# Differential attention of a two-model kernel: the next pair's row maxima directly behind a pair's normalisations on VectorE

## The reference

```python
def diff_attend(q, k, v, lam):
    s = jnp.einsum("bhmqd,bhmkd->bhmqk", q, k).astype(jnp.float32) * (DIFF_QK_DIM ** -0.5)
    p = jax.nn.softmax(s, axis=-1)
    w = (p[:, :, 0] - lam * p[:, :, 1]).astype(v.dtype)
    return jnp.einsum("bhqk,bhkd->bhqd", w, v)
```

## Time and profile before

| | us |
|---|---|
| median of 3 runs | 2204.16 |
| lowest, highest run | 2200.81, 2211.51 |
| the profiled execution's own time | 2201.68 |
| its span in the trace | 2199.8 |
| TensorE busy, share of the span | 2100.1, 95% |
| VectorE busy | 1562.9, 71% |
| ScalarE busy | 1031.1, 47% |
| GpSimd busy | 312.9, 14% |
| mean granted TensorE clock | 0.991 |

### The profile page before, as it was taken

The page is one execution under the profiler, slowest core; times in us unless marked ns, Lnnn a source line. Parts: engine busy times, 40 slices in busy tenths (PEclk is TensorE's granted clock), DMA queues, the critical chain, the costliest instruction groups (busy, mean ns, idle before and its releaser), DMA issues.

```text
span 2199.8 us, 41515 instructions
## 1 busy us (share of the span) xinstructions
PE 2100.1 (95%) x17009; PEld 1973.0 (90%) x17009; DVE 1562.9 (71%) x2072; ACT 1031.1 (47%) x1238; POOL 312.9 (14%) x292
## 2 busy tenths in 40 slices
PE   7899999899899999999999889999999988999998
PEld 6676898799899999999999878999999987899998
DVE  8988657688787655655579988675556998875554
ACT  4112636554664543534545556563355446544332
POOL 3762003200210100100201220110010122000000
PEclk9999999999999999999999999999999999999999
DMA  8688766665445565555666433555555642345552
GB/s 258 226 296 302 256 243 218 219 186 186 122 133 173 188 194 189 176 191 191 200 184 194 129 97 107 176 174 191 188 176 179 186 142 85 108 154 172 181 182 77
DMA packets 292260, 397.42 MB, mean 181 GB/s; under 512 B 9270, under 2 KB 257292, under 8 KB 285452
## 3 DMA queue, kind: packets, MB, share of 16 engines
q1 hardware_dynamic: 285620, 383.53, 53.4%
q0 software_dynamic: 3008, 5.56, 1.1%
q10 hardware_dynamic: 3480, 6.18, 0.8%
HBM read 387.53 MB, written 3.15 MB: 178 GB/s over the span
## 4 chain that ended last, share of the span: by engine, by line
PE 77%; DVE 13%; issue 3%; ACT 3%; DMA 2%; POOL 1%; DVEq 0%; SPq 0%; ACTq 0%; POOLq 0%
PE L L941 63%; PE M L941 4%; DVE w_rest L454 3%; PE L L1222 2%; PE L L1208 2%; PE M L1476 1%; PE L L1235 1%; DVE work L2783 1%; PE L L1291 1%; DMA raw<-in_w_in 1%; POOL m L862 1%; DMA gate<-in_mem 1%; ACT w_high L448 1%; DVE n_rest L2204 1%; PE M L1075 1%
## 5 line engine op out<-in xcount | busy, mean ns | idle before, releaser
L941 PE MATMUL L<-n_high,w_high 128*128 128x256 f32 x3104 | 875.7, 282 | 15.7 <-DVE w_rest L454 10.0
L941 PE MATMUL L<-n_rest,w_high 128*128 128x256 f32 x3104 | 865.9, 279 | 0.0
L941 PE MATMUL L<-n_high,w_rest 128*128 128x256 f32 x3104 | 865.9, 279 | 0.0
L454 DVE TENSOR_TENSOR w_rest<-raw,w_high 128x2048 fp32r<-128x2048 f32 x293 | 673.7, 2301 | 215.6 <-PE L L941 200.6
L448 ACT ACTIVATE w_high<-raw 128x2048 fp32r<-128x2048 f32 x293 | 561.1, 1916 | 342.6 <-PE L L941 316.1
L941 PEld LDWEIGHTS L<-n_high,w_high 128*128 128x128 f32 x3104 | 587.1, 189 | 33.3 <-issue 17.7
L941 PEld LDWEIGHTS L<-n_high,w_rest 128*128 128x128 f32 x3104 | 586.3, 189 | 0.0
L941 PEld LDWEIGHTS L<-n_rest,w_high 128*128 128x128 f32 x3104 | 584.8, 188 | 0.0
L941 PE MATMUL L<-hid_high,w_high 128*128 128x256 f32 x768 | 214.4, 279 | 4.2 <-DVEq L2689 4.2
L941 PE MATMUL L<-hid_high,w_rest 128*128 128x256 f32 x768 | 213.7, 278 | 0.0
L941 PE MATMUL L<-hid_rest,w_high 128*128 128x256 f32 x704 | 195.8, 278 | 0.0
(11 more groups left out here) (426 smaller groups left out, 2962.0 us busy)
## 6 DMA issues: line engine op xcount, KB each, us to landing
raw<-in_w_in SPq DMA_DIRECT2D x116, 1024.0 KB, 5.5
raw<-in_w_ffn SPq DMA_DIRECT2D x99, 1024.0 KB, 5.3
raw<-in_w_ada SPq DMA_DIRECT2D x32, 1024.0 KB, 6.6
raw<-in_w_out SPq DMA_DIRECT2D x16, 1024.0 KB, 4.9
raw<-in_w_gate SPq DMA_DIRECT2D x11, 1024.0 KB, 5.4
raw<-in_w_up SPq DMA_DIRECT2D x11, 1024.0 KB, 5.4
raw<-in_w_down SPq DMA_DIRECT2D x11, 1024.0 KB, 4.9
work<-in_w_ada SPq DMA_DIRECT2D x8, 1024.0 KB, 7.3
```

The lines of the kernel that those rows point to most:

```text
L454: nc.vector.tensor_tensor(w_rest[:, u.first % 2, :], raw[:, u.first % 4, :], w_high[:, u.first % 4, :].bitcast(F32), ALU.subtract).then_in ...
L941: ins = mm(dst, a, b, start=first and i == 0, stop=last and i == 2, skip_group_check=skip)
```

## The change

```diff
                     if kind_of(key) == "diff":
                         if x["whole"]:
-                            for y in tasks[i + 1:i + 3]:
+                            turned_rest(x)
+                        else:
+                            for y in tasks[i + 2:i + 4]:
                                 negative_max(key, y)
-                            turned_rest(x)
```

## The result

The changed kernel takes **2226.56 us** (median of 4 runs, 2225.57 to 2230.45), the kernel before 2206.05 beside it (4 runs): ratio 1.0096, 95% interval 1.0072 to 1.0121, some 20.5 us slower. The profiled execution took 2227.25, its span is 2225.5. Forecast were 2218, in a range from 2208 to 2227, so the time lies at its upper end: 20.5 us more than before, where the sum had 14.2. The sign and the places were right, the size was not.

What follows compares the result with a forecast made beforehand. VectorE's order was taken to set the pace inside differential attention stages. Terms of 8.6 + 3.6 + 2.0 = 14.2 us on the profiled 2201.7 gave 2215.9, and 2.5 us more for the median gave 2218, range 2208 to 2227.

Steps and rivals of the forecast that it cites:

- What bounds, and where it goes: Differential attention stages: VectorE's order can set the pace; maxima moved ahead of their scores make VectorE and what follows wait.
- Pair 1, 2.0 + 2.9 + 3.7 = 8.6: `conv_centre` behind pair 1's maxima starts late by 2.0 us in c0diff, 2.9 in x0diff, 3.7 in x1diff.
- Pair 2, 1.15 + 1.2 + 1.2 = 3.6: `w_rest`, head copy and `conv_scale` behind the maxima delay head 1's values: 1.15 us in c0diff, 1.2 per 512-key stage.
- The term on the overlap with GpSimd: Pair 2: later `conv_scale` leaves part of its overlap with GpSimd's subtractions, giving back 0.5 us per 512-key stage.
- Pairs 4 and 5, 0.65 in each: `w_rest` behind the maxima makes head 2's values 0.65 us later in each stage, 2.0 us in all.
- Pair 0, nothing: `w_rest` behind two maxima costs nothing; pair 1's exponentials start 2.2 us sooner but gain nothing.
- The clock, "I count 0 net": Slow clock behind new waits before the second sums, set against head 2's shorter wait: 0 net, 5 us as the end.
- Rival (a): The clock also falls behind the new waits: +5 us, 2223; chance 0.20.
- The reason given for a return: Head 2's wait gets shorter, since 2.3 us of waiting moved ahead of it, and such a wait can cost clock.
- Rival (b): Only `conv_centre`'s delay arrives, partly absorbed; pairs 2 to 5 cost nothing: +7 us, 2211; chance 0.18.
- Rival (c): Exponentials are the pace, and `w_rest` leaves their chain at pairs 0, 4, 5: 8 us faster, 2196; chance 0.06.

Runs made afterwards that it cites:

- f2: Kernel before with only pair 1's maxima directly behind its normalisations, so that only `conv_centre` goes behind them: ratio 1.0058, three stages +14.0 us.
- g1: Changed kernel with extra matmuls that fit inside TensorE's waits behind the turnings of pairs 1 and 4: ratio 1.0070 to the kernel before, three stages +15.0 us.
- g2: Kernel before with early maxima in pair 2 alone: ratio 1.0032, three stages +8.4 us.
- h1: Kernel before with early maxima in pairs 4 and 5 alone: ratio 1.0025, three stages +11.3 us.
- g3: Kernel before with early maxima in pairs 0 and 5 alone: ratio 0.9965, three stages -5.0 us.
- f3: Kernel before with early maxima in pair 4 alone: ratio 0.9980, three stages +0.6 us.
- g4: Kernel before with early maxima in pairs 0 and 5, and pair 5's rest part ahead of `w_rest`: 2192.1 us, ratio 0.9955, three stages -8.8 us.
- i1: g4 with 10 extra matmuls ahead of pair 0's turning in x0diff and x1diff: ratio 0.9961 to the kernel before, three stages -8.3 us.

## Why the prediction was right or wrong

**What bounds, and where it goes: right.** VectorE's order set the pace, the scores were 1.0 us behind their first matmul, and each wait named stands in the profile near its number (`b_sq` 3.21, 3.53, 3.53 us; `w_rest` 1.6 and 2.99; head 2 2.21).

**Pair 1, 2.0 + 2.9 + 3.7 = 8.6: right.** f2 has 2.0, 2.9 and 2.7, in all 7.7. x1diff was overstated by 1.0. The row it was read from the earlier trace rows has pair 2's scores 8.8 us behind the first turning, at a clock of 0.71 up to there; in f2 they stand 7.9 us behind it, as in x0diff (8.0 before). A slow stretch of one profile was taken for a property of the stage.

**Pair 2, 1.15 + 1.2 + 1.2 = 3.6: near, in part by luck.** In the changed kernel it is 1.72, 0.69 and 0.68, 3.1 in all. The term on the overlap with GpSimd was mis-sized there, in both directions. `conv_scale` now takes 1.79 us in c0diff (1.22 before) and 1.38 in x0diff (2.33 before).

So 0.95 us came back in a 512-key stage, not 0.5, and 0.57 were lost in c0diff. 1.7 - 0.95 = 0.75 and 1.15 + 0.57 = 1.72: the delays themselves were right. In g1 and g2 `w_rest` is 0.57 us longer, as the prediction had expected ("while `w_rest` enters it"), 0.95 - 0.57 = 0.38 come back, and pair 2 costs 1.3 us in x1diff. Which of the two happens hangs on the moment.

**Pairs 4 and 5, 0.65 in each: right for the 512-key stages without the clock.** From head 1's values to head 2's g1 is 1.3, 0.7 and 0.7 us longer than before, in all 2.8 against 2.0; c0diff was given the 512-key stages' number and costs twice that. The chain from pair 6's scores over `w_rest` to the rest part is what h1 shows.

**Pair 0, nothing: wrong by a little, and on the other side.** The earlier maxima are worth something where TensorE waited for the convolution: in g3 c0diff's second sums came 1.0 us earlier. The step "then waits for the convolution, not for a pair: gain nothing" missed that the convolution's `conv_centre` stands on VectorE behind pair 1's normalisations, which do come earlier. In the changed kernel pair 1's maxima cover this.

**The clock, "I count 0 net": this step failed.** The delays sum to 14.2 us in the prediction and to 15.0 in g1, where the waits for `b_sq` and for pair 4's `w_rest` are filled. That these two are so close is partly luck: by its parts g1 has 9.3 up to the second sums, 5.3 from head 0's values to head 1's (1.6 more in x0diff than in the changed kernel: the longer `w_rest`, and the clock behind the unfilled wait), 2.8 to head 2's, and 2.5 less behind them, where the clock no longer falls. The changed kernel loses 7.0 more: from the second sums to head 0's values 1.15 in each 512-key stage, from head 1's values to head 2's 1.5, 1.7 and 1.6, and behind head 2's values 1.5 and 1.4 in the 512-key stages, 10.0 in all, less 3.0 by which g1 is the longer one in the stretches between. Rival (a), with a chance of 0.20 and 2223 us, was the mechanism that happened, at 7 instead of 5 us. The reason given against it, that the new waits are shorter than 4.1 us, does not hold in the 512-key stages: waits of 2.99 and 3.53 us were followed by a clock of 0.65 to 0.72. In c0diff the wait of 3.21 us was followed by a whole clock in the changed kernel and by a slow one in f2 (4.78 us from the sums to head 0's values instead of 3.22), so how much is lost at one place is not fixed by the length of the wait. The reason given for a return, that head 2's wait gets shorter, holds with pair 4 alone (f3) and fails with pair 5 early as well (h1). The Trainium skill ("TensorE: Matmul & The Clock Gate", "Part 1: The HAM clock gate") has the throttled clock as the default, which activity releases; what the prediction drew from it, that each new wait is paid twice, pointed the right way. The 5 us were too small, since they were counted for the waits in front of the sums alone and not for those for `w_rest`.

**Rival (b)**, `conv_centre` alone, is out: g2 shows pair 2's cost. **Rival (c)** fell for the changed kernel, but its condition was the right one: the change pays where the scores are done before VectorE is. It holds at pair 5 as well as at pair 0: pair 6's scores start at 1281.81 and are done 1.0 us later, and VectorE ends pair 5's normalisations only near 1283.7, where TensorE's turning has waited 1.00 us for them. The prediction looked at pairs 0, 2 and 4 alone.

**What stays open.** Pair 1 (14.0), pair 2 (8.4) and pairs 4 and 5 (11.3) sum to 33.7 us, the whole to 22.0. 5.3 of the 33.7 are the clock behind head 2's values in x1diff in f2's and g2's profiles, which the old order can lose too. That delays overlap, and that one slow stretch can be filled by another's wait, is the likely reason; it was argued, not run. What decides whether the clock falls behind one and the same wait in one profile and not in another was not looked into; it moves a stage by up to some 3 us (f2's and g2's x1diff). Why the rest of the program varies by 13 us between executions was not looked into.

## What to carry to other kernels

An instruction on an in-order engine may be taken forward only to where its input is already there; otherwise it carries its wait in front of all that it overtook, so ask at each place separately, and expect the answer to differ from pair to pair (g4, with two places of eight, is faster than both kernels). Price a new wait of TensorE twice, its length and the slow clock that may stand behind it, and check whether a later wait pays for either, and whether that later wait moves along. Parts that are harmless alone may not be so together. Before a stage of one profile is compared with one of another, compare their granted clocks: the same order gave 54.7 and 56.3 us.

## What the hardware showed

- In the changed kernel's x0diff the waits of 3.53 and 2.99 us were each followed by a slow clock (0.65, 0.72): 4.85 us instead of 3.7 for the same matmuls, 6.03 instead of 4.28. With extra matmuls of no use in these waits the granted clock behind them was 1.00. Shorter waits can do it too, and not always: 2.18 us in g1's x0diff (0.67) but 2.17 in its x1diff (1.00); and 3.21 us in c0diff was followed by 1.00 in the changed kernel.
- A call that multiplies float32 operands as they are (128x256) is recorded as two matmuls, 0.216 us apart, so 13 calls take 5.8 us.
- Clock that is won back gains little if another engine is next: in i1's x0diff the sums came 0.6 us sooner than in g4's, behind a new wait of 0.80 us, and the stage was 0.1 us shorter.
- VectorE's 128x1024 `conv_scale` took 1.22, 1.38, 1.79 or 2.33 us with the same operands, by its moment. In x1diff before (2.33) it started 0.05 us behind a GpSimd subtraction of 1.29 us, in the changed kernel (1.37) 0.3 us before the end of one and 0.3 us ahead of the next. That these subtractions are the cause is a reading of the timeline and was not tested.
